# Hyena input projection in one unrolled block, with both operands split into two fp32r parts

## What is computed

```python
def hyena_mixer(h, o, P):
    z = h @ P['hy_w_in'][o]                      # (tokens, 1024) @ (1024, 3072)
    cw = P['hy_conv_w'][o]
    z = cw[0] * shift_prev(z) + cw[1] * z + cw[2] * shift_next(z) + P['hy_conv_b'][o]
    x0, x1, v = jnp.split(z, 3, axis=-1)
    ...
    y = long_conv((v * x1).astype(F32), h_f, h_b, P['hy_skip'][o].astype(F32))
    return (y.astype(h.dtype) * x0) @ P['hy_w_out'][o]
```

## Time and profile before

| | |
|---|---|
| median of 3 runs | 4687.15 us (4679.49 to 4689.08) |
| span of the profiled execution | 4686.8 us |
| TensorE matmul busy | 4067.4 us (87%) |
| TensorE weight load busy | 3246.8 us (69%) |
| VectorE busy | 3519.9 us (75%) |
| ScalarE busy | 1527.0 us (33%) |
| GpSimd busy | 1661.4 us (35%) |

### The profile page before, as it was taken

One profiled execution on the slowest core, in us unless ns is written; L12 is line 12 of the kernel. 1 busy time (PEld: TensorE's weight loads), 2 busy tenths in 40 slices (PEclk: granted clock), 3 DMA queues, 4 the chain that ended last, 5 costly groups with the idle time before them and its releaser, 6 DMA issues. The chain is left out here.

```text
span 4686.8 us, 79149 instructions
## 1 busy us (share of the span) xinstructions
PE 4067.4 (87%) x29098; PEld 3246.8 (69%) x29098; DVE 3519.9 (75%) x7180; ACT 1527.0 (33%) x2923; POOL 1661.4 (35%) x1279
## 2 busy tenths in 40 slices
PE   6779999968947999999999389889587999999994
PEld 1346666655935899999999255349567999999994
DVE  3225666644898899999999633436997999999998
ACT  1124444422238333333333211012194333333332
POOL 0001111111320466666666300011402666666665
PEclk8889999989979999999999699899799999999997
DMA  8620000012006999999999211230048999999996
GB/s 339 238 74 17 19 19 19 17 58 102 2 1 191 388 407 403 406 406 399 394 395 396 110 50 44 68 120 16 1 121 312 407 398 407 406 405 390 391 398 233
DMA packets 391821, 1050.68 MB, mean 224 GB/s; under 512 B 37111, under 2 KB 168439, under 8 KB 388344
## 3 DMA queue, kind: packets, MB, share of 16 engines
q0 software_dynamic: 147456, 536.94, 29.1%
q1 hardware_dynamic: 217144, 494.64, 28.1%
q10 hardware_dynamic: 27008, 16.25, 1.2%
HBM read 992.16 MB, written 55.54 MB: 224 GB/s over the span
## 5 line engine op out<-in xcount | busy, mean ns | idle before, releaser
L873 PE MATMUL bank<-h_parts,u_parts 128*128 128x384 f32 x6144 | 1116.7, 336 | 40.5 <-DVE u_parts L968 36.8
L873 PEld LDWEIGHTS bank<-h_parts,u_parts 128*128 128x128 f32 x6144 | 1081.5, 188 | 62.2 <-issue 37.2
L883 PE MATMUL bank<-v_parts,gg_parts 128*128 128x512 f32 x4608 | 1100.2, 392 | 10.4 <-DVE v_parts L988 10.4
L883 PEld LDWEIGHTS bank<-v_parts,gg_parts 128*128 128x128 f32 x4608 | 862.8, 188 | 184.5 <-issue 13.2
L851 POOL DMA_INDIRECT late<-in_peer_v,rows_idx x512 | 618.9, 1209 | 197.7 <-issue 152.4
L957 DVE SCALAR_TENSOR_TENSOR late<-late,yT 128x1024 f32<-128x1024 f32 x512 | 660.2, 1291 | 32.8 <-DMA late<-in_peer_v,rows_idx 18.8
L924 ACT ACTIVATE gg_parts<-late 128x384 fp32r<-128x384 f32 x256 | 133.7, 522 | 1034.3 <-DVE late L978 1023.0
L843 POOL DMA_INDIRECT late<-in_u_rows,rows_idx x256 | 348.1, 1360 | 303.6 <-DVE yT L951 282.0
L843 POOL DMA_INDIRECT hT<-in_u_rows,rows_idx x128 | 212.8, 1662 | 486.3 <-DVE h_parts L943 360.2
L947 DVE TENSOR_TENSOR u_parts<-hT,u_parts 128x1024 fp32r<-128x1024 f32 x256 | 311.5, 1217 | 44.4 <-issue 25.8
L488 PE MATMUL bank<-hT,late 128*128 128x128 f32 x2560 | 315.2, 278 | 8.4 <-PEq L60 8.4
(11 more groups left out here) (350 smaller groups left out, 5691.2 us busy)
## 6 DMA issues: line engine op xcount, KB each, us to landing
yT<-in_peer_v SPq DMA_DIRECT2D x256, 512.0 KB
hT<-in_peer_u SPq DMA_DIRECT2D x256, 512.0 KB
w_modt<-in_w_mod SPq DMA_DIRECT2D x24, 2048.0 KB, 15.3
late<-gates SPq DMA_DIRECT2D x168, 192.0 KB
late<-in_peer_wq SPq DMA_DIRECT2D x32, 512.0 KB, 12.4
gates<-late SPq DMA_DIRECT2D x2, 8192.0 KB, 30.4
gates<-gates_sb SPq DMA_DIRECT2D x2, 8192.0 KB, 30.4
w_hy<-in_hy_w_in SPq DMA_DIRECT2D x9, 1536.0 KB, 6.8
```

The source lines that it names most:

```text
L873: mm = pe.matmul(m.bank[j % 2][:, 0:TD], us[:, j % 2, a, k, :], hs[:, b, k, :], start=(k == 0 and i == 0), stop=(k == KD - 1 and i == 2))
L883: mm = pe.matmul(yb[t][c][:, :], gs[:, j, a, t * P:(t + 1) * P], vs[:, j % 2, b, c * BANK:(c + 1) * BANK], start=(first and i == 0), stop= ...
```

## The change

`hyena_inputs` becomes one block without a loop, over N = 24 projections n = 3 d + q:

- `project(n)`: each fp32 matmul becomes three fp32r products, high weights by high h, high by low, low by high (`PARTS`). The 640 tokens are taken as two halves of 320 columns, in two banks, so a projection has 8 x 3 x 2 = 48 matmuls, with three pairs of banks in turn. It waits for the low weights of n and, from n = 3, for the copy of n - 3 out of its banks.
- The parts: ScalarE copies the weights of n (128x1024) to fp32r, VectorE subtracts to get the low part; two slots. Once, at the start, both make the parts of `m.hT`, eight steps of 128x640 each.
- SyncE loads the weights in pieces of 512 KB, one for each n, two slots; piece n waits for the low part of n - 2. The columns' load goes out after piece 1, the DFT table after piece 3.
- `padded(n)` copies three pieces (128, 192 and 320 columns) instead of two. `turn(d)` stands after projection 3 d + 3, the last one at the end. `u` is written straight into `H.u`.
- One set of semaphores, cleared once, at the end. `H.ut` and `H.tab` are allocated one level further out.

The diff, with the old version of the engines' lists left out:

```diff
 def hyena_inputs(nc, m, H):
+    N = 3 * KD
+    HALF = T // 2
+    PARTS = ((0, 0), (0, 1), (1, 0))
     with ExitStack() as ctx:
-        w = buf(ctx, nc, "w_hy", P, 2, 3, KD, P)
-        us = buf(ctx, nc, "u_turn", P, 2, T)
+        raw = buf(ctx, nc, "w_raw", P, 2, KD, P)
+        ws = buf(ctx, nc, "w_parts", P, 2, 2, KD, P, dtype=F32R)
+        hs = buf(ctx, nc, "hy_parts", P, 2, KD, T, dtype=F32R)
         cols = buf(ctx, nc, "hy_cols", P, KD, NHC)
         zp = buf(ctx, nc, "zp_hy", P, 3, ZW)
         c1 = buf(ctx, nc, "conv", P, 3, T)
+        s = sems(ctx, nc, "hi_cols", "hi_tab", "hi_zero", "hi_w0", "hi_w1", "hi_hhi", "hi_hlo", "hi_whi", "hi_wlo",
+                 "hi_mm", "hi_zp", "hi_chain", "hi_conv", "hi_u", "hi_tr", "hi_ut")
-        with nc.Fori(0, KD // 2) as pair:
-            with nc.Block() as block:
...
         with nc.Block() as block:
             @block.sync
             def _(sp):
+                for n in range(N):
+                    if n >= 2:
+                        sp.wait_ge(s["hi_wlo"], n - 1)
+                    sp.dma_start(raw[:, n % 2], m.i["hy_w_in"][n // 3][:, n % 3]).then_inc(s[f"hi_w{n % 2}"], 16)
+                    if n == 1:
+                        sp.dma_start(cols[:, :, :], m.i["hy_cols"]).then_inc(s["hi_cols"], 16)
+                    if n == 3:
+                        sp.dma_start(H.tab[:, :, :, :], m.i["dft"]).then_inc(s["hi_tab"], 16)
+                sp.wait_ge(s["hi_tab"], 16)
             @block.gpsimd
             def _(pool):
+                pool.memset(zp[:, :, :], 0.0).then_inc(s["hi_zero"], 1)
+                pool.wait_ge(s["hi_zero"], 1)
+
+            @block.tensor
+            def _(pe):
+                def project(n):
+                    pe.wait_ge(s["hi_wlo"], n + 1)
+                    if n >= 3:
+                        pe.wait_ge(s["hi_zp"], n - 2)
+                    for k in range(KD):
+                        if n == 0:
+                            pe.wait_ge(s["hi_hlo"], k + 1)
+                        for i, (a, b) in enumerate(PARTS):
+                            for half in range(2):
+                                mm = pe.matmul(m.bank[2 * (n % 3) + half][:, 0:HALF], ws[:, n % 2, a, k, :], hs[:, b, k, half * HALF:(half + 1) * HALF],
+                                               start=(k == 0 and i == 0), stop=(k == KD - 1 and i == 2))
+                    mm.then_inc(s["hi_mm"], 1)
+
+                def turn(d):
+                    pe.wait_ge(s["hi_u"], d + 1)
+                    if d >= 1:
+                        pe.wait_ge(s["hi_ut"], d)
+                    for t in range(TT):
+                        mm = pe.transpose(m.bank[6 + t // 4][:, (t % 4) * P:(t % 4 + 1) * P], H.u[:, d, t * P:(t + 1) * P], m.ident[:, :])
+                    mm.then_inc(s["hi_tr"], 1)
+
+                for n in range(N):
+                    project(n)
+                    if n >= 3 and n % 3 == 0:
+                        turn(n // 3 - 1)
+                turn(KD - 1)
+
+            @block.scalar
+            def _(act):
+                def weights(n):
+                    act.wait_ge(s[f"hi_w{n % 2}"], 16 * (n // 2 + 1))
+                    act.activation(ws[:, n % 2, 0], raw[:, n % 2], ACT.Copy).then_inc(s["hi_whi"], 1)
+
+                def padded(n):
+                    q = n % 3
+                    a, b = m.bank[2 * q], m.bank[2 * q + 1]
+                    if n >= 3:
+                        act.wait_ge(s["hi_conv"], n - 2)
+                    act.activation(zp[:, q, ZOFF[0]:ZOFF[0] + T_CTX], a[:, 0:T_CTX], ACT.Copy)
+                    act.activation(zp[:, q, ZOFF[1]:ZOFF[1] + HALF - T_CTX], a[:, T_CTX:HALF], ACT.Copy)
+                    act.activation(zp[:, q, ZOFF[1] + HALF - T_CTX:ZOFF[1] + T_LAT], b[:, 0:HALF], ACT.Copy).then_inc(s["hi_zp"], 1)
+
+                def turned(d):
+                    act.wait_ge(s["hi_tr"], d + 1)
+                    act.activation(H.ut[:, 0:4, d * P:(d + 1) * P], m.bank[6][:, :].rearrange("p (t n) -> p t n", t=4), ACT.Copy)
+                    act.activation(H.ut[:, 4, d * P:(d + 1) * P], m.bank[7][:, 0:P], ACT.Copy).then_inc(s["hi_ut"], 1)
+
+                weights(0)
+                for k in range(KD):
+                    act.activation(hs[:, 0, k], m.hT[:, k, :], ACT.Copy).then_inc(s["hi_hhi"], 1)
+                weights(1)
+                act.wait_ge(s["hi_zero"], 1)
+                for n in range(N):
+                    act.wait_ge(s["hi_mm"], n + 1)
+                    padded(n)
+                    if n + 2 < N:
+                        weights(n + 2)
+                    if n >= 4 and n % 3 == 1:
+                        turned(n // 3 - 1)
+                turned(KD - 1)
+                act.wait_ge(s["hi_ut"], KD)
+
+            @block.vector
+            def _(dve):
+                link = linker(dve, s["hi_chain"])
+
+                def weights(n):
+                    dve.wait_ge(s["hi_whi"], n + 1)
+                    dve.tensor_tensor(ws[:, n % 2, 1], raw[:, n % 2], ws[:, n % 2, 0].bitcast(F32), ALU.subtract).then_inc(s["hi_wlo"], 1)
+
+                def convolve(n):
+                    d, q = n // 3, n % 3
+                    col = lambda c: cols[:, d, c:c + 1]
+                    dve.wait_ge(s["hi_zp"], n + 1)
+                    for step, (off, tap) in enumerate(((0, 1), (-1, 0), (1, 2))):
+                        for c, a, width in SEGS:
+                            z = ZOFF[c] + off
+                            src, weight = zp[:, q, z:z + width], col(HC_TAPS + 3 * q + tap)
+                            dst = c1[:, q, a:a + width]
+                            if step == 0:
+                                ins = dve.tensor_scalar(dst, src, weight, col(HC_BIAS + q), ALU.mult, ALU.add)
+                            elif step == 2 and q == 0:
+                                ins = dve.scalar_tensor_tensor(H.x0[:, d, a:a + width], src, weight, dst, ALU.mult, ALU.add)
+                            else:
+                                ins = dve.scalar_tensor_tensor(dst, src, weight, dst, ALU.mult, ALU.add)
+                            if step < 2 or c == 0:
+                                link(ins)
+                    ins.then_inc(s["hi_conv"], 1)
+                    dve.wait_ge(s["hi_conv"], n + 1)
+                    if q == 2:
+                        dve.tensor_tensor(H.u[:, d], c1[:, 1], c1[:, 2], ALU.mult).then_inc(s["hi_u"], 1)
                         dve.wait_ge(s["hi_u"], d + 1)
+
+                weights(0)
+                for k in range(KD):
+                    dve.wait_ge(s["hi_hhi"], k + 1)
+                    dve.tensor_tensor(hs[:, 1, k], m.hT[:, k, :], hs[:, 0, k].bitcast(F32), ALU.subtract).then_inc(s["hi_hlo"], 1)
+                weights(1)
+                dve.wait_ge(s["hi_cols"], 16)
+                for n in range(N):
+                    if n >= 1 and n + 1 < N:
+                        weights(n + 1)
+                    convolve(n)
...
             H.x0 = buf(middle, nc, "x0", P, KD, T)
+            H.ut = buf(middle, nc, "ut", P, TT, D)
+            H.tab = buf(middle, nc, "dft", P, TT, 2, T_LAT)
+            hyena_inputs(nc, m, H)
             H.y = [m.hT[:, :, :].rearrange("p k t -> p (k t)").rearrange("p (t d) -> p t d", d=D), buf(middle, nc, "y_sin", P, TT, D)]
-            with ExitStack() as inner:
-
-                H.ut = buf(inner, nc, "ut", P, TT, D)
-                H.tab = buf(inner, nc, "dft", P, TT, 2, T_LAT)
-                hyena_inputs(nc, m, H)
-                hyena_spectra(nc, m, H)
+            hyena_spectra(nc, m, H)
             hyena_back(nc, m, H)
```

More of the change, by code:

```diff
@@ L2232, in _ @@
+                sp.wait_ge(s["hi_tab"], 16)
             @block.gpsimd
             def _(pool):
-                pool.memset(zp[:, :, :], 0.0).then_inc(c0["hi_zero"], 1)
-                pool.wait_ge(c0["hi_zero"], 1)
-        s = sems(ctx, nc, "hi_w0", "hi_w1", "hi_mm", "hi_zp", "hi_chain", "hi_conv", "hi_u", "hi_tr", "hi_ut")
-        with nc.Fori(0, KD // 2) as pair:
-            with nc.Block() as block:
[L2239 to L2272, removed]
-                    for d in range(2):
-                        act.wait_ge(s["hi_u"], d + 1)
-                        act.activation(pick(H.u[:, :, :], 2 * pair + d), us[:, d], ACT.Copy)
-                        act.wait_ge(s["hi_tr"], d + 1)
-                        col = bass.ds((2 * pair + d) * P, P)
-                        act.activation(H.ut[:, 0:4, col], m.bank[6][:, :].rearrange("p (t n) -> p t n", t=4), ACT.Copy)
-                        act.activation(H.ut[:, 4:5, col], m.bank[7][:, 0:P].rearrange("p (t n) -> p t n", t=1), ACT.Copy).then_inc(s["hi_ut"], 1)
-                    act.wait_ge(s["hi_ut"], 2)
-                @block.vector
[L2283 to L2291, removed]
-                                    z = ZOFF[c] + off
-                                    src, tap = zp[:, q, z:z + width], col(HC_TAPS + 3 * q + n)
-                                    dst = c1[:, q, a:a + width]
```

(13 more changed lines are left out.)

6 lines of the change are left out of this document (removed).

## The result

The changed kernel takes 4607.45 us, the median of 4 runs (4605.67 to 4609.39), beside 4686.54 us for the kernel before in its 4 runs. The ratio is 0.9832, with a 95% interval of 0.9821 to 0.9844: 1.7% faster. In five more runs on another chip it took 4604.84 us, beside 4684.93. The forecast was 4615.7 us, with a range of 4600 to 4642.

The account below looks back on a forecast made before the run. TensorE and the gaps between turns bound the input projection; matmuls 37.2, drains and restarts 28.8 less 1.7, and other starts 7 save 71.5 us, so 4687.15 becomes 4615.7 us, range 4600 to 4642.

Parts of the forecast that it names:

- What bounds the stage: Input projection before the change: bound by TensorE plus what stands between turns; the function lasts 265.7 us.
- Matmuls: Projection matmuls of 320 columns: 148 ns each, a tile 7.10 instead of 8.65 us, 24 tiles 170.4 instead of 207.6.
- the two bounds: Limits on a 320-column matmul: 174.6 ns (no gain below 384 columns, +31 us) and 133.3 (columns alone, -17 us).
- The slower rival: Projection weight loads don't hide: a matmul would be 321 ns, the time 4815 us; chance 0.02.
- The start: First DMA at 2671.65 to tile 0's end at 2688.4: data landed in 3.4 us, 6.1 us at the lower clock.
- The steady part: After tile 0, no drains between tiles: 23 x 7.10 = 163.3 us plus 3.9 of transposes, last projection ending at 2855.6.
- The tail: Last projection to next stage: 10.7 us before, three pieces add 0.1, one closing clear less takes off about 0.5.
- The cover: Weight preparation on ScalarE and VectorE stays hidden behind TensorE's matmuls, with slack 1.0 us, and 0.7 for q = 2.
- rival of 133.3 ns: Projection matmuls cost nothing beside their columns; preparation then limits, 12 of 17 us remain: 4604 us; chance 0.06.
- The sum: Whole function, 71.5 us saved: matmuls 37.2, three drains and restarts 28.8 less 1.7 for transposes, other 7.
- its 7: Remaining saving in the function, 7 us: cold starts of turns 2 to 4 and the earlier start.
- the runs' own spread: Variation of the whole time between runs, some 5 us, counted in the forecast's own range 4606 to 4626.

Follow-up runs that it names:

- run with two products: The changed kernel without the product of high weights and low h, 32 matmuls a projection instead of 48, all parts still made: 4562.87 us (0.9734).
- fp32 block: The changed kernel's single block without parts, using fp32 matmuls of 512 and 128 columns: 4645.45 us, ratio 0.9917 to the kernel before.

## Why the prediction held, point by point

**What bounds the stage.** Right: TensorE and the drains between turns. With both cut, the function shrank by 28%.

**Matmuls.** Forecast 148 ns, measured 146.7 (7.04 us for 48). The estimate drew a line through 384 and 512 columns; the two bounds, 133.3 and 174.6, both fell. The two rows lie 14.6 and 15.6 ns above their columns, where the prediction had 14 for both; at 320 it is 13.4. The line was luckier than it looked, since 128 columns cost 111 to 113 ns. The Trainium skill ("TensorE: Matmul & The Clock Gate", Back-to-back issue gap) gives N/2.4 + 2.5 ns for a warm matmul taken by itself. This trace does not agree for fp32r: 135.8 ns would have been 11 too low, and at 384 columns the rows of before are 12 ns above it.

**The slower rival.** It had the weight loads stand in line. The matmuls start 146.7 ns apart, each with a load of its own, and a load's record is 190 ns long, so they do not. The Trainium skill ("TensorE: Matmul & The Clock Gate", The mechanism) has the sentence that the prediction used, that a weight load overlaps matmuls in flight only when the row group differs, and the trace disagrees. The same section also lets a load into the background weight buffer go ahead, which the prediction left out.

**The start.** Forecast 16.75 us from the first DMA to the end of projection 0; the first read comes at 17.2. ScalarE had its data 4.1 us in, where 3.4 was expected, and the lower clock lasted some 5.4 us, not 6.1.

**The steady part.** Forecast 167.2 us for 23 steps and seven turns. From the first read at 2681.18 to the last at 2846.82 it is 165.6, 1.6 less, of which the matmul's 1.3 ns makes 1.4.

**The tail.** Forecast 10.3, from the last projection's end to the next stage. The order of time of the changed kernel:

```profile
2846.82 0.28 ACT L2286 ACTIVATE zp_hy<-bank 128x128 f32<-128x128 f32 x1 [5.55 <-PE bank L2257]
...
2851.95 1.33 PE L2266 MATMUL bank<-ident,yT 128*128 128x128 f32 x5 [5.16 <-DVE yT L2338]
...
2853.81 0.27 ACT L2293 ACTIVATE ut<-bank 128x128 f32<-128x128 f32 x1
...
2855.92 4.61 PE L2379 MATMUL bank<-ut,dft 128*128 128x512 f32 x5 [2.65 <-PEq L60]
```

9.1 us from the read, or 9.3 from the projection's end. From the last copy to the next stage it is 1.8 us. At the end of the loop it was 2.9, from this copy to 2937.36:

```profile
2934.21 0.27 ACT L2279 ACTIVATE ut<-bank 128x128 f32 x1
```

So 1.0 is saved where 0.5 was taken: a mis-sized term.

**The cover.** Forecast slack 1.0 us, and 0.7 behind q = 2. In the trace TensorE never waits for low weights after tile 0, and they are ready 1.4 to 2.0 us before it comes, 1.0 behind q = 2. The run with two products reaches 5.4 us a tile. The prediction's rival of 133.3 ns took the chain for the limit at 6.1 to 7 us a tile and so left 12 of 17 us; by the runs 48 such matmuls, 6.4 us, would still have hidden it, so that price was too small.

**The parts of the gain.** The sum gave 37 for matmuls and 34 for the rest. Measured with the fp32 block between the two: 34.5 and 39.3. The matmul term itself was right, 37.2 from the first read to the last; the parts of the start take 2.7 of it back. In the 39.3, the first read of the banks comes 6.0 us earlier (14.5 instead of 20.6 us after the function's start) and the tail is 1.5 shorter. That leaves 31.8 us for three drains with their restarts, net of the 1.7 us of transposes, where the sum had 28.8 - 1.7 and a share of its 7. The two misses had opposite signs, so part of the close total is luck.

**The time.** 8.3 us below the forecast: 2.3 us by the function, the rest outside it. The step that was off is the sentence that what is saved in the function comes off the span whole, and nothing else changes. In the profiles the changed kernel's function starts 7.7 us earlier than in the one profile of before that the sum used, whose prologue was one of the long ones (209.0 us against 203.2). The median of before holds executions of both kinds, as far as four profiles tell; none of the two of after was long. The prediction gave the runs' own spread 5 us, and a range of 42 us hid the rest.

## What to carry to other kernels

When fp32 matmuls are split into three fp32r products, look at the narrow tiles: of the 34.5 us that the parts brought here, 27 hang on cutting 640 columns into two equal pieces instead of 512 and 128. An estimate from the rows: an fp32 matmul of 128 columns is two records of 0.11 us, and three fp32r products of 128 columns would be three times 0.11, so at that width the parts would lose. A loop whose body drains pays its whole latency chain and a restart at the lower clock each turn (10 to 11 us here); with the start and the tail that was worth as much as the parts. And when the time varies by 10 us between executions, compare the length of the changed stage in the traces, which repeats to 1 us.

## What the runs showed of the hardware

- fp32r matmuls at 2.4 GHz start 146.7 ns apart at 320 columns, 174.6 at 384 and 229 at 512, each with a weight load whose record is 190 ns long; a pair of 512 and 128 columns takes 340. At 1.2 GHz it is some 267 ns at 320 columns and 320 at 384, with nothing on top of the columns.
- After a drain of 8 us TensorE is at 1.2 GHz again: a granted clock of 0.54 over the next 3.9 us after one drain, 0.50 over 4.5 us after the next and over 3.4 us after the third, in the same code.
- The prologue, the same code, took 203 or 212 us in two executions of one kernel on one chip. The granted clock between 68 and 88 us was 0.99 in the short one and 0.50 in the long one, and the same 16 matmuls took 1.90 and 3.59 us.
